# Each slot of an expert gather fetched as two half rows: one gather for the dot product, one for the added values

## The reference, cut to what matters

```python
act = jax.nn.gelu(jnp.einsum('td,thkd->thk', tb, u_tab[ib]).astype(jnp.float32))
return jnp.einsum('thk,thkd->td', (gb * act).astype(tb.dtype), v_tab[ib])
```

## Time and profile before

| | |
|---|---|
| Median of 3 runs | 2476.83 us (2469.85 to 2478.46) |
| The profiled execution | 2471.97 us, its span 2470.2 us |
| Gathers | 768, 1292 ns each on POOL in the mean |
| Dot products (DVE) | 768, 1226 ns each |
| Read from HBM | 935.88 MB, of it 805.36 MB by gathers |
| DMA packets by POOL's queue | 110592 |
| Granted TensorE clock, mean | 0.96 |

### The profile page before, as it was taken

The page is one execution under the profiler, slowest core; times in us unless marked ns, Lnnn a source line. Parts: engine busy times, 40 slices in busy tenths (PEclk is TensorE's granted clock), DMA queues, the critical chain, the costliest instruction groups (busy, mean ns, idle before and its releaser), DMA issues.

```text
span 2470.2 us, 23913 instructions
## 1 busy us (share of the span) xinstructions
PE 2116.3 (86%) x6856; PEld 1125.4 (46%) x6856; DVE 1559.2 (63%) x3849; ACT 937.2 (38%) x2734; POOL 1027.7 (42%) x868
## 2 busy tenths in 40 slices
PE   6988898799999989888899898787688987777777
PEld 4864544345565535443365453335455532222222
DVE  2247877765646669867747878353578887544444
ACT  1014443343334444434454335233343544333333
POOL 0013244454444454434444444320133545677774
PEclk9999999899999999999999999997699999999999
DMA  9629999999999999999999999982199999999997
GB/s 405 272 93 387 369 417 421 421 421 421 421 421 417 409 421 417 421 418 414 421 421 414 390 419 411 421 339 70 68 369 374 413 421 422 421 422 421 422 421 329
DMA packets 132305, 938.36 MB, mean 380 GB/s; under 512 B 14688, under 2 KB 17760, under 8 KB 18656
## 3 DMA queue, kind: packets, MB, share of 16 engines
q0 software_dynamic: 110592, 805.36, 79.1%
q1 hardware_dynamic: 21600, 131.63, 13.2%
HBM read 935.88 MB, written 1.05 MB: 379 GB/s over the span
## 4 chain that ended last, share of the span: by engine, by line
PE 44%; DMA 22%; DVE 13%; POOL 8%; issue 8%; ACT 4%; POOLq 0%; SPq 0%; DVEq 0%; ACTq 0%
PE psum L779 22%; DMA uv<-uv_dram,stage_idx 20%; PE psum L593 11%; POOL uv L834 8%; PE psum L575 6%; DVE uv L1333 5%; PE psum L524 1%; PE psum L725 1%; DMA wring<-ada_dram 1%; ACT diag L983 1%; DMA uv<-ada_dram 1%; ACT wv L981 1%; PE psum L685 1%; PE psum L753 1%; ACT gel L979 0%
## 5 line engine op out<-in xcount | busy, mean ns | idle before, releaser
L779 PE MATMUL psum<-uv,diag 128*128 128x512 f32 x3072 | 1470.5, 619 | 255.7 <-ACT diag L983 250.6
L834 POOL DMA_INDIRECT uv<-uv_dram,stage_idx x768 | 992.4, 1292 | 1121.2 <-PE psum L779 906.5
L1333 DVE CUSTOM_DVE_ANT_0 uv<-uv,h 128x1024 f32<-128x1024 f32 x768 | 933.1, 1226 | 530.2 <-DMA uv<-uv_dram,stage_idx 521.5
L779 PEld LDWEIGHTS psum<-uv,diag 128*128 128x128 f32 x3072 | 566.1, 194 | 1047.5 <-ACT diag L983 525.2
L979 ACT ACTIVATE gel<-dots 128x1 f32<-128x1 f32 x768 | 154.8, 202 | 1053.6 <-DVE dots L1333 1052.6
L983 ACT ACTIVATE diag<-const,wv 128x128 f32<-128x128 f32 x768 | 308.3, 401 | 25.0
L593 PE MATMUL psum<-hT,wring 128*128 128x256 f32 (+1 forms) x1280 | 280.8, 374 | 0.0
L593 PEld LDWEIGHTS psum<-hT,wring 128*128 128x128 f32 x1280 | 238.7, 195 | 61.2 <-issue 34.1
L981 ACT ACTIVATE wv<-gel,gw 128x1 f32<-128x1 f32 x768 | 226.3, 295 | 24.9
L826 POOL COPY stage_idx<-idx 128x8 uint32 x96 | 35.1, 366 | 298.3 <-DVE idx L1305 297.7
L856 ACT ACTIVATE work<-psum 128x256 f32<-128x256 f32 (+2 forms) x126 | 51.6, 410 | 201.8 <-PE psum L593 134.1
(11 more groups left out here) (174 smaller groups left out, 1280.4 us busy)
## 6 DMA issues: line engine op xcount, KB each, us to landing
wring<-ada_dram SPq DMA_DIRECT2D x35, 1024.0 KB, 9.6
wring<-in_dram SPq DMA_DIRECT2D x26, 1024.0 KB, 9.2
wring<-wq_dram SPq DMA_DIRECT2D x24, 1024.0 KB, 9.0
uv<-ada_dram SPq DMA_DIRECT2D x13, 1024.0 KB, 18.7
uv<-uv_dram,stage_idx POOLq DMA_INDIRECT x768, 14.1
uv<-in_dram SPq DMA_DIRECT2D x8, 1024.0 KB, 21.9
wring<-out_w_dram SPq DMA_DIRECT2D x5, 1024.0 KB, 9.1
wring<-out_dram SPq DMA_DIRECT2D x4, 1024.0 KB, 7.6
```

The source lines that it names most:

```text
L779: last = mm(acc[:, b, :], diag[:, s % RING, :], uv[:, s % RING, D + 512 * b:D + 512 * (b + 1)], start=(c == 0), stop=(c == NSEL - 1))
L834: nc.gpsimd.indirect_dma_start(out=uv[:, s, :], out_offset=None, in_=tables[stage // 2], in_offset=bass.IndirectOffsetOnAxis(ap=stage_idx[ ...
L1333: v.tensor_tensor_reduce(out=uv[:, r, 0:D], in0=uv[:, r, 0:D], in1=h2[:, stage % 2, t, :], scale=1.0, scalar=0.0, op0=ALU.mult, op1=ALU.ad ...
```

## The change

The tables u and v are kept apart in HBM, each with rows of 4 KB. Each slot is now fetched by two gathers: one of u rows into the first half of the place in `uv`, one of v rows into the second half, each with its own semaphores, `u_landed` and `v_landed`. The first waits for `dots_ready`, that is for the dot product of the slot eight before, the second for `uv_used` as the single one did. DVE waits for `u_landed`, PE for `v_landed` as well. Since a dot product can now be made before PE has used the place, `dots`, `gel` and `wv` get sixteen places, and ACT waits for `uv_used` ahead of `diag`, which keeps eight. `dots_ready` starts at 8.

```diff
-        dots, gel, wv = (sb(s, [P, RING]) for s in ("dots", "gel", "wv"))
+        dots, gel, wv = (sb(s, [P, 2 * RING]) for s in ("dots", "gel", "wv"))
...
-        uv_landed = [sem(f"uv_landed{i}") for i in range(RING)]
+        u_landed = [sem(f"u_landed{i}") for i in range(RING)]
+        v_landed = [sem(f"v_landed{i}") for i in range(RING)]
...
+                pe.wait_ge(v_landed[s % RING], 16 * (s // RING + 1))
                 pe.wait_ge(diag_ready, s + 1)
...
-            tables = [A["uv0"], A["uv1"]]
+            tables = [(A["u0"], A["v0"]), (A["u1"], A["v1"])]
...
-                        pool.wait_ge(uv_used, it * TOPK + (T * NSEL + half * RING + s + 1))
-
+
+                        u, v = tables[stage // 2]
+                        pool.wait_ge(dots_ready, it * TOPK + (T * NSEL + half * RING + s + 1))
                         pool.sem_inc(slot_claimed, 1)
                         nc.gpsimd.indirect_dma_start(
-                            out=uv[:, s, :], out_offset=None, in_=tables[stage // 2],
+                            out=uv[:, s, 0:D], out_offset=None, in_=u,
                             in_offset=bass.IndirectOffsetOnAxis(ap=stage_idx[:, half, s:s + 1], axis=0),
-                        ).then_inc(uv_landed[s], 16)
+                        ).then_inc(u_landed[s], 16)
+                        pool.wait_ge(uv_used, it * TOPK + (T * NSEL + half * RING + s + 1))
+                        pool.sem_inc(slot_claimed, 1)
+                        nc.gpsimd.indirect_dma_start(
+                            out=uv[:, s, D:2 * D], out_offset=None, in_=v,
+                            in_offset=bass.IndirectOffsetOnAxis(ap=stage_idx[:, half, s:s + 1], axis=0),
+                        ).then_inc(v_landed[s], 16)
...
-                act.wait_ge(dots_ready, s + 1)
+                act.wait_ge(dots_ready, RING + s + 1)
...
-                f(diag[:, r, :], C("ident"), ACT.Copy, scale=wv[:, r:r + 1]).then_inc(diag_ready, 1)
+
+                act.wait_ge(uv_used, s + 1)
+                f(diag[:, s % RING, :], C("ident"), ACT.Copy, scale=wv[:, r:r + 1]).then_inc(diag_ready, 1)
...
-                dve.wait_ge(uv_landed[r], 16 * (s // RING + 1))
+                dve.wait_ge(u_landed[r], 16 * (s // RING + 1))
...
+            dve.sem_inc(dots_ready, RING)
...
-        "uv0": np.concatenate([f(peer_u)[0], f(peer_v)[0]], 1),
-        "uv1": np.concatenate([f(peer_u)[1], f(peer_v)[1]], 1),
+        "u0": f(peer_u)[0], "v0": f(peer_v)[0], "u1": f(peer_u)[1], "v1": f(peer_v)[1],
```

More of the change, by code:

```diff
@@ L975, in weigh @@
             def weigh(s):
-                T, c, r = s // NSEL, s % NSEL, s % RING
-                act.wait_ge(dots_ready, s + 1)
+                T, c, r = s // NSEL, s % NSEL, s % (2 * RING)
+                act.wait_ge(dots_ready, RING + s + 1)
                 f(gel[:, r:r + 1], dots[:, r:r + 1], ACT.Gelu_apprx_tanh).then_inc(gelu_ready, 1)
@@ L1331, in dot @@
                     dve.wait_ge(*taken["h2", stage, t])
-                dve.wait_ge(uv_landed[r], 16 * (s // RING + 1))
+                dve.wait_ge(u_landed[r], 16 * (s // RING + 1))
                 v.tensor_tensor_reduce(out=uv[:, r, 0:D], in0=uv[:, r, 0:D], in1=h2[:, stage % 2, t, :], scale=1.0, scalar=0.0,
-                                       op0=ALU.mult, op1=ALU.add, accum_out=dots[:, r:r + 1]).then_inc(dots_ready, 1)
+                                       op0=ALU.mult, op1=ALU.add, accum_out=dots[:, s % (2 * RING):s % (2 * RING) + 1]).then_inc(dots_ready, 1)
             def close(T):
```

## The result

| | before | after |
|---|---|---|
| Median | 2473.34 us (2468.59 to 2478.46) | 2628.39 us (2618.62 to 2633.85) |
| Ratio, with its 95% interval | 1 | 1.0622 (1.0581 to 1.0663) |
| The profiled execution, its span | 2471.97, 2470.2 us | 2633.85, 2632.1 us |
| Granted TensorE clock, mean | 0.96 | 0.95 |

The change costs 155 us, 6.2%. The forecast was 2762 us, the range 2590 to 2935: slower as said, inside the range, but with little more than half of the cost that was forecast.

The account below looks back on a forecast made before the run. Transfers and PE bound the kernel before, POOL following; split gathers put POOL in front. 768 slots x 3.13 us = 2404, plus 324 outside, 45 excess, less 18, plus 1.8 and 5: 2762 us, range 2590 to 2935.

Parts of the forecast that it names:

- A half gather costs as much as a whole: On POOL, each gather of half rows was taken at 0.93 us, with 0.30 us to the next.
- Base: POOL's two undisturbed gather starts a slot: 2 x 1.24 = 2.48 us, or 2.58 with copies of row numbers.
- Rival (B): Transfers and PE stay the bound, as half gathers cost about half or slip between dot products: 2500 or 2520 us; chance 0.07.
- (D): Faster: cheap half gathers and earlier freeing keep the queue fed in slow blocks, about 2440 us; chance 0.02.
- The stall: POOL gathers starting under DVE's dot product are held 0 to 1.10 us; taken as 0.55 us a slot.
- two self-feeding cadences: Dot product locks onto first-half starts (stall 0.29 us) or second-half starts (0.91); both in turn, mean 0.60.
- copies: POOL's copies of row numbers, one in 8 slots, lengthen the gap between gathers: 0.10 us a slot.
- waits for other engines: Sixteen of 94 blocks of eight slots are slower for reasons of PE and DVE: 45 us of excess.
- outside the slots: Time before the first gather, between stages 1 and 2 and after the last gather starts: 324 us, less 18 saved.
- the saving that was expected between stages 1 and 2: At the end of stage 1 a shallower queue lands gathers sooner after issue, saving 9 us.
- PE's wait for v: PE waiting for the second half's landing: hidden, or 0.1 us of delay that adds to no cadence.
- (C): The dot product lands badly nearly always and the clock falls: stall 1.10, 3.68 us a slot, 3150 us; chance 0.06.

Follow-up runs that it names:

- e1: The changed kernel with its waits, order and rings, but one gather of 8 KB rows a slot again: 2473.89 us, 1.0019 of the kernel before.
- e5: The changed kernel with v fetched in two gathers of 2 KB rows, three gathers a slot: 3662.71 us, 1.482 of the kernel before.
- e2: The changed kernel with three quarters of v left out, v rows of 1 KB: 2688.46 us, 1.0893 of the kernel before.
- e9: The changed kernel again, nothing edited, in a later measurement: 2710.90 us, 1.0976 of the kernel before.
- e3: The changed kernel with the dot product replaced by a one-input sum over u's row: 2673.14 us, 1.082 of the kernel before.
- e4: The changed kernel with v rows of 1 KB and a one-input sum for the dot product: 2659.01 us, 1.075 of the kernel before.
- e11: The changed kernel with the dot product over 512 of 1024 values, still two inputs: 2683.82 us, 1.0851 of the kernel before.
- e13: The changed kernel a third time, nothing edited: 2617.03 us, 1.0597 of the kernel before.
- e12: The kernel before with 13 ACT increments a slot of a semaphore nobody waits for: 2517.29 us, 1.0177 of the unedited one.
- e8: The kernel before with the dot product replaced by a one-input sum over u's row: 2469.53 us, 0.9987 of the unedited one.

## Why the prediction was right or wrong

**What bounds the kernel: right.** It said that transfers, PE and POOL stand side by side, and that POOL goes to the front once its slot takes over 2.49 us. e1 (POOL back to one gather, time back to 1.002) and e5 (a third gather, 1.48) show it from both sides, and e2 that the bytes don't do it. It is cleanest in stage 2; in stages 0 and 1 the slots took 2.89 us before, so that 3.03 costs only 0.14 us a slot.

**A half gather costs as much as a whole: right.** Shortest 932 ns, median 940; at 2 KB and 1 KB (e5, e2) the shortest is 940 to 942. Base 2.48 us, as measured. Rival (B), cheap halves, falls with it, and (D), faster, too.

**The stall: right in its rule, too large in size.** This is the step that failed. The prediction argued from an arbitrary phase, corrected it upwards to 0.60 by two self-feeding cadences, and took 0.55; measured are 0.33. The number of starts under a dot product was right: by the trace 46% of the gathers, 0.92 a slot, for "about one of the two". But those are held for only 0.33 us in the mean, where half of 1.10 was assumed. At an arbitrary phase the stalls would be spread evenly from 0 to 1.10; of the 615 gathers that took over 0.96 us, 307 were held by less than 0.3 and 104 by 0.8 or more. In stage 2 the timeline shows how that can come about. The dot product of 1.23 us fits almost exactly between two starts 1.24 us apart, as at 2351.77 above. A stretch without a stall then runs at 2.49 us, somewhat faster than the landings come (dot products 2.55 apart at 2363.41 and 2365.96, by the trace), so the dot product slips slowly over a start, small stalls first; each stall pushes the starts away from it again. This explanation is read from a few microseconds of stage 2 and was not tested by a run. In stages 0 and 1, where DVE has much else to do, the stall is as small (0.31 and 0.35 us a slot, for 0.34 in stage 2), so the phase isn't arbitrary there either, and nothing here says why. e2's 0.39 and e5's 0.42 show only that the size can move.

**The fixed terms.** Against the forecast for the profiled execution, 2757 us, 2634 were measured, 123 less:

| Term | difference |
|---|---|
| stall, 768 x (0.33 - 0.55) | -169 us |
| copies, 768 x (0.127 - 0.10) | +21 us |
| waits for other engines, 61 for the 45 of excess | +16 us |
| outside the slots, 315 for 306 | +9 us |

The last one is the saving that was expected between stages 1 and 2: it didn't come (132.0 us from gather to gather there, by the trace, for 131.8 before). The one at the kernel's end did, as the last slot's first gather starts 15.8 us ahead of the span's end for 24.7.

**What was said to be free: right.** PE's wait for v (339.4 of PE's 384.3 us of idle time there still end with ACT's `diag`), ACT's wait, the rings, the clock (0.99 in the last stretch, so (C) is out). The transfers of 4 KB rows ran at 411 GB/s, for the 410 of the earlier trace rows.

**What to see in the profile: half right.** Idle time ended by "issue", DVE waiting for u, 346 to 370 GB/s in stage 2: all there. "POOL busy over 80%" was wrong by its own numbers: two gaps of 0.30 in 3.1 us leave about 80% at most, and no digit is above 7. Gathers of 1.10 us lay just under the 1.15 to 1.35 named, the same error as the stall's. Landings were said to take some 5 us and took 7.7: 10.2 and 10.7 in stages 0 and 1, where the transfer engines are still full, and 6.2 in stage 2 (medians by the trace).

**What no step of it had: late increments.** They are 6 us in after, of the 61 above, but 66 us in e9. And the counterfactual on which the size of the stall term rests, that without a stall the kernel would be some 250 us faster, isn't shown: e3, e4 and e11 took the stall away or most of it and got at most 52 us back, 27 in the one pair on one chip, with the late increments in all three.

**Left open.** What makes the increments of `uv_used` arrive late. The traces with late increments lack a good part of their semaphore records: 20299 are left in e9, while after and e13, the same program, have 35149 and 35151. All runs with two or three gathers a slot on the chips of e1, e4 and e9 lack records so (e2 has 21189), and all have some late waits, e2 the least, 20 us. Even the kernels with one gather a slot lack 1 or 2% of them on the first two of these chips (21655 in e1 for 22101 in the kernel before), and e12, with 32077 on e13's chip, lacks next to none. So the chip or the occasion is one rival, the number of updates a second, the two together a third; whether the recording itself has a part, no run tells. The batches come about 15 slots apart and drift against POOL's loop of 16 slots, so the loop isn't what sets the 43 us. Two runs would part these and weren't made: e3 or e11 beside e13 on its chip, and the changed kernel with half its updates. So of the 155 us, the base and the stall are measured on POOL as busy time; that a kernel without the stall would be faster by its size is argued only, and the runs without the stall had another wait in its place.

No version that was tried beats the kernel before beyond its interval: with a base of 2.58 us on POOL for two gathers, against 2.49 for the transfers, there is no room for one.

## What to carry to other kernels

Before splitting a DMA, count what its issuing engine pays for a start, the gap included (here 1.24 us, whatever the size of the rows), and set the number of starts per period against the period; an engine that is busy for 42% and waits most of the rest can become the bound by one such split. Measure first what a deeper ring would bring by making it one place shallower: here that was 0.5%, by estimate more than earlier freeing of half a place could bring. And where a cost depends on how two engines' instructions fall against each other, the arbitrary phase is only a guess: compare the length of the one with the spacing of the other, for at a near match long stalls can be the rare ones, as here. And measure a kernel again, unchanged, beside its variants: this one moved by 94 us from one measurement to the next, more than any edit moved it that kept its two gathers.

## What the runs showed of the hardware that was not expected

- A gather of 128 rows takes POOL 0.93 to 0.94 us undisturbed (shortest) at 8, 4, 2 and 1 KB a row, and the next starts 0.30 us later.
- A gather that starts while DVE runs an instruction with two SBUF inputs that writes 1024 values a partition back to SBUF ends 0.81 us behind it; with one input and a single value written (e8, e3) there is nothing of this. A gather that has already started is not held, and DVE isn't slowed either way (1226 and 1218 ns).
- An increment of a semaphore that stands by itself takes ACT's queue 0.068 us (e12, 13 in a row). In a ring of eight places without slack one late slot comes back every eighth slot, 0.65 us late, to the end of the stage.
- The same program took 2617, 2628 and 2711 us in three measurements (2617 and 2711 on different chips), beside a kernel before that stayed the same; the longest one has longer waits for a semaphore. In e3 such a wait ended 15.4 us after the work it was for, as six increments arrived within 0.32 us. A difference of under 94 us between two variants of the changed kernel needs both in one measurement.
